# Page gathers of the sample cache spread over seven heads, and the first gate activation moved ahead in the weight loop

## What is computed

```
h = rms_norm(x, norm_pre);  z = h @ w_in      # c_q, c_kv, k_r, u_pool, u_conv, gate
o_lat = attend(q_abs, q_rope, c_kv, k_r)      # 8 heads; for the samples also over
                                              #   cache_ckv[page_table], cache_krope[page_table]
mixed = concat([o_att, y_pool, y_conv]) * silu(gate)
out   = x + rms_norm(mixed @ w_out, norm_post)
```

## Time and profile before

| | |
|---|---|
| median of 3 runs | 1404.8 us (1403.98 to 1406.93) |
| the profiled execution | 1409.98 us, of which 1408.2 us are the span |
| busy over the span | PE 91%, PE weight loads 75%, DVE 59%, ACT 44%, POOL 34% |
| stage 2 | about 455 to 944 us |
| stage 3 | 944 to 1010 us |
| stage 4 | 1010 us to the end |

### The profile page before, as it was taken

How to read it: one execution, slowest core, us unless ns; L and a number is a source line. 1 busy time by engine, 2 the same in 40 slices (tenths; PEclk the granted TensorE clock), 3 DMA queues, 4 the chain that set the end, 5 groups by cost and what they waited for, 6 DMA issues and landing times. The chain is left out here.

```text
span 1408.2 us, 21384 instructions
## 1 busy us (share of the span) xinstructions
PE 1285.1 (91%) x7456; PEld 1058.7 (75%) x7456; DVE 836.8 (59%) x1799; ACT 625.4 (44%) x1271; POOL 483.9 (34%) x420
## 2 busy tenths in 40 slices
PE   4889979989865899999999999959889999999998
PEld 3767758677534788888888888856568888888885
DVE  3468676686663888888888888834334232333312
ACT  5423142341421777777777777724242222221211
POOL 5236146352362235234152350008603232222312
PEclk9999999999975899999999999979999999999999
DMA  7534161241516032231231321637263131313221
GB/s 244 150 101 152 40 213 64 91 166 50 198 32 117 10 102 67 74 92 36 81 95 40 91 56 30 190 90 208 94 213 119 62 120 61 120 60 120 75 64 38
DMA packets 141696, 141.71 MB, mean 101 GB/s; under 512 B 55637, under 2 KB 110902, under 8 KB 140118
## 3 DMA queue, kind: packets, MB, share of 16 engines
q1 hardware_dynamic: 133350, 112.19, 27.2%
q0 software_dynamic: 5360, 17.68, 4.3%
q10 hardware_dynamic: 2880, 10.49, 2.3%
HBM read 104.08 MB, written 46.71 MB: 107 GB/s over the span
## 5 line engine op out<-in xcount | busy, mean ns | idle before, releaser
L1291 ACT ACTIVATE pT<-tp 128x512 fp32r<-128x512 f32 (+2 forms) x320 | 168.4, 531 | 116.9 <-PE tp L1230 107.9
L1348 DVE TENSOR_SCALAR_CACHE_REDUCE prob<-sc 128x512 f32<-128x512 f32 (+2 forms) x320 | 192.9, 603 | 31.6 <-PE sc L1222 17.7
L1357 DVE TENSOR_TENSOR big<-tp,pT 128x512 fp32r<-128x512 f32 (+2 forms) x320 | 193.9, 607 | 28.2 <-ACT pT L1291 27.8
L2006 PE MATMUL m<-w_gate,q2a 128*128 128x512 f32 x768 | 181.8, 396 | 3.5 <-POOLq L1984 3.5
L1230 PE MATMUL tp<-ident,prob 128*128 128x128 f32 x1088 | 171.9, 273 | 1.1 <-DVE big L1357 1.1
L1281 ACT ACTIVATE prob<-prob,nm 128x1024 f32<-128x1024 f32 (+2 forms) x192 | 171.7, 894 | 1.2 <-DVE nm L1351 0.7
L2006 PEld LDWEIGHTS m<-w_gate,q2a 128*128 128x128 f32 x768 | 145.5, 191 | 33.6 <-POOLq L1984 3.6
L701 DVE SCALAR_TENSOR_TENSOR acc<-aT,cols,acc 128x512 f32<-128x512 f32 x232 | 163.1, 751 | 10.2 <-DVE qst L777 0.9
L2168 DVE SCALAR_TENSOR_TENSOR shared<-m,rq,g_post 128x512 f32<-128x512 f32 x32 | 22.6, 747 | 232.0 <-POOL rq L1978 232.0
L1230 PEld LDWEIGHTS tp<-ident,prob 128*128 128x128 f32 x1088 | 128.8, 141 | 25.1 <-issue 1.7
L894 PE MATMUL mm<-big,w_in 128*128 128x512 f32 x576 | 141.8, 404 | 5.1 <-ACTq L585 5.1
(11 more groups left out here) (291 smaller groups left out, 2303.6 us busy)
## 6 DMA issues: line engine op xcount, KB each, us to landing
xtok<-in_x ACTq DMA_DIRECT2D x20, 512.0 KB, 4.5
xraw<-in_xT SPq DMA_DIRECT2D x17, 512.0 KB, 4.4
QT<-qst SPq DMA_DIRECT2D x32, 256.0 KB, 3.4
LAT<-in_cache_ckv SPq DMA_DIRECT2D x128, 64.0 KB, 2.1
k2a<-Y SPq DMA_DIRECT2D x16, 512.0 KB, 5.5
shared<-in_x SPq DMA_DIRECT2D x16, 512.0 KB, 4.4
out_y<-shared SPq DMA_DIRECT2D x16, 512.0 KB, 2.9
raw<-QT SPq DMA_DIRECT2D x7, 1024.0 KB, 5.1
```

The source lines that it names most:

```text
L1291: act.activation(pT[0][:, 4 * c:4 * c + w // P, (t % 4) * P:(t % 4 + 1) * P], tp[n % NTP][:, 0:w].rearrange("p (k q) -> p k q", q=P), ACT. ...
L1348: dve.tensor_scalar(prob[:, slot[m % J], 0:w], sc[b][:, 0:w], -1.0, None, ALU.mult, ALU.min, accum_out=top).then_inc(sc_free[b], 1)
L1357: dve.tensor_tensor(cut(1), tp[n % NTP][:, 0:w].rearrange("p (k q) -> p k q", q=P), f32(cut(0)), ALU.subtract)\
L2006: last = pe.matmul(out, w(pw_, k), x(px, k), start=(k == 0 and q == 0), stop=(k == n - 1 and q == 2))
```

## The change

The 128 pages are numbered through, over all samples, and dealt over 28 slots, the four groups of heads 0 to 6. A slot has 4 or 5 pages, head 7 none. The wait ahead of `load_first_pages` is now for all pages. In stage 4, `silu(0, 0)` and `divide(0)` stand ahead of chunk 2 instead of chunk 4.

```diff
-                def gather(b, pages):
-
-                    for pg in pages:
+                def gather(pages):
+
+                    for b, pg in (divmod(n, N_PAGES) for n in pages):
...
-                        parts = 4 if h < HEADS - 1 else 2
-                        if g < parts:
-                            gather(h, range(g * N_PAGES // parts, (g + 1) * N_PAGES // parts))
+                        at, slots = h * 4 + g, 4 * (HEADS - 1)
+                        if at < slots:
+                            gather(range(at * DEC_BATCH * N_PAGES // slots, (at + 1) * DEC_BATCH * N_PAGES // slots))
...
-                            sp.wait_ge(s["gather"], 32 * (DEC_BATCH - 1) * N_PAGES)
+                            sp.wait_ge(s["gather"], 32 * DEC_BATCH * N_PAGES)
...
                 for k in range(MC):
-                    if k == MC // 2:
+                    if k == MC // 4:
                         silu(0, 0)
...
                 for k in range(MC):
-                    if k == MC // 2:
+                    if k == MC // 4:
                         divide(0)
```

## The result

The changed kernel takes 1397.5 us (median of 4 runs, 1396.1 to 1398.4), against 1405.9 us for the kernel before. The ratio is 0.9943, with a 95% interval of 0.993 to 0.9956: 8.0 us faster, between 6.2 and 9.8. The forecast was 7.9 us.

A forecast was written before the change was run, and what follows sets the result against it. It took TensorE's nearly unbroken stage 4 stream to set the end, with holes in head 7 and at stage 4's start. -9.92 - 1.1 + 0 + 0.9 + 2.2 = -7.9 us, from 1404.8 to 1396.9 us; range 1392.0 to 1401.5.

The forecast's parts named there:

- Gathers out of head 7: Stage 2, head 7: without 8 pages ahead of group 0's store, VectorE's wait goes whole, -9.92 us, plus -1.1 us.
- the second term: Head 7: TensorE's lower clock behind the idle time goes too, -1.1 us, taken from between 0 and 2.
- The store isn't too late behind the loads: Head 7: group 0's store lands by 908.4 us, needed at 913.53; rival of a late store, 1401.9 us, chance 0.10.
- Heads 0 to 6 cost nothing: Stage 2: 16 more pages in heads 0 to 6 are covered, cost 0; without cover 32 us.
- V's gap on SP: Head 2: SP has 4.47 us between group 0's store and issuing V, covering a slot's growth of 2.03 us.
- the slower rival: Heads 0 to 6: longer slots delay V and TensorE waits, 1429 us, from 4.47 us of growth; chance 0.04.
- The silus: Start of stage 4: silus end 4.6 us earlier, but the output projection of tile 0 starts later and slower, +3.1 us.
- The slow stretch: Stage 4: after some 8 us idle, TensorE starts tile 0's output projection at half clock, +2.2 us.
- a gain of 7.4 us: Stage 4 rival: Y's load lands early enough that the gates' end decides, up to -7.4 us, 1386.4 us; chance 0.05.
- The offset: Whole kernel: the profiled execution lies 5.2 us above the median of the runs, taken as constant.
- the last two rivals: Longer slots delay V, 1429 us, chance 0.04; head 7's wait has another cause than SP's order, 1408 us, 0.02.
- the slower side: Whole kernel: chance that the change measures slower, given as 0.05.

The follow-up runs named there:

- silus_only: Kernel before with both silus moved ahead of chunk 2, nothing else: 1410.5 us, ratio 1.0025.
- hole_filled: Changed kernel with 30 unneeded matmuls added on TensorE between the gates of tile 1 and the first output projection: 1395.5 us, ratio 0.9921.
- four buffers: Changed kernel with silus back ahead of chunk 4 and the chunks of w_out loaded through four buffers instead of two: 1390.2 us, ratio 0.9881.
- four_buffers_early: Changed kernel, silus ahead of chunk 2, with four buffers for the chunks of w_out instead of two: 1395.7 us, ratio 0.9912.
- gathers_only: Changed kernel with both silus back ahead of chunk 4, so only the gathers are moved: 1397.2 us, ratio 0.9935 to the kernel before.
- slots_four_heads: Changed kernel with silus back ahead of chunk 4 and gathers dealt over four heads, 16 slots of 8 pages: 1446.95 us (one run).
- stores_before_gathers: Kernel before with each group's store in head 7 issued ahead of that group's page gathers: 1405.0 us, ratio 0.9991.
- slots_five_heads: Changed kernel with silus back ahead of chunk 4 and gathers dealt over five heads, 20 slots of 6 or 7 pages: 1396.1 us (one run).

## Why the prediction was right, and where it wasn't

**Gathers out of head 7: right.** Forecast -9.92 - 1.1 us, measured 10.9 to 11.0 us less of head 7 in each kernel that leaves no page there. That the second term came out is luck: I took 1.1 us from between 0 and 2, and no row fixed it. Two kernels tell the cause from its rivals: the wait goes when the store is put first, and comes back with 2.0 us when 4 pages are put ahead of it.

**The store isn't too late behind the loads: right, with less to spare than I had worked out.** SP gets to it at 899.80 us, 9.2 us ahead of the `ost` of group 2. I took 4.0 us for its landing, from the first gather, and it took 5.7 behind the 5 MB of loads. The reserve was 3.5 us instead of 5.1. The wait went whole all the same, so the sum wasn't hurt.

**Heads 0 to 6 cost nothing: right in the sum, wrong in its reason.** They take 425.6 to 427.9 us with the 28 slots and 427.1 to 427.4 without. The limit wasn't V's gap on SP: 7 pages passed it, for one wait of 1.2 us in the whole stage. What decides, as far as two kernels can tell, is whether SP's whole load fits into a head of 57.5 us: with 52 us of gathers it does, with 65 it takes 69 and doesn't, and the stores feel it first. My point of decision for the slower rival, 4.47 us of growth, was wrong.

**The silus: right.** They ended earlier, the hole moved behind the gates (8 us forecast, 7.85 measured), and the part costs. Forecast +0.9 and +2.2 us; measured +0.7 and +1.9 between the two kernels, and 2.3 us between the means over all. silus_only gives it by the time alone, 3.5 us (2.0 to 5.1). The slow stretch is shown by hole_filled. The later start of 0.7 us isn't, since it varies by 1.6 us between kernels with the same order, and its working was off: counted from the first gate matmul, SP issues the load of `Y` 1.6 us later (24.6 and 23.0 us), not 0.9, and it then lands 0.8 us sooner behind its issue. I named the load of `Y` as the thing that the projection waits for. It is the last to end, but taking it away gains nothing, since the chunks' chain ends only 0.9 us ahead of it. Of the rivals, a gain of 7.4 us was excluded because that chain had no slack, and with four buffers, where it has, the gain is there.

**The offset: wrong.** I took the 5.2 us between the profiled execution and the median as constant. It was mostly variation in stage 1: the changed kernel's profiled execution lay 0.6 us above its median, at 1398.1 us instead of the forecast 1402.1. The sum was made of differences within a stage, so it wasn't hurt. The cuts of the two traces give -11.0 + 2.6 = -8.4 us and the runs 8.0, between 6.2 and 9.8, so the forecast's 7.9 can't be told from either. A slip on the way: the last two rivals have 0.04 and 0.02, and I gave the slower side 0.05.

## What to carry to other kernels

An issuing engine that works in program order is a resource: count its time per step, and look for small urgent stores queued behind many transfers that have no hurry; then spread these over all steps that have room, since merely reordering them leaves their sum. Moving a wait up in an engine's order helps only if the work put behind it isn't what the next consumer waits for; before it is moved, ask which chain ends second, and by how little. And TensorE's idle time can cost twice: here 3.7 to 8.4 us of it at the start of stage 4 brought 1.6 to 2.7 us more at the lower clock, while up to 2.0 us brought nothing.

## What the runs showed of the hardware

- Behind 7.85 us of idle the granted clock stayed at 0.50 for about 4 us (changed kernel). A shorter hole wasn't cheaper: in four_buffers_early, with 3.69 us, the clock fell at 1027 us, about 1 us ahead of the projection, and stayed at 0.50 until 1033.8, 5.6 us behind the projection's start, and cost 2.6 us where the longer one cost 1.9. Across 0.75, 1.5 and 2.0 us of idle (gathers_only, hole_filled, slots_four_heads) it stayed at 1.00. Thirty matmuls of no use, 6.96 us long, won 1.9 us.
- Identical code in stage 1 ended anywhere between 447.5 and 455.7 us over twelve profiled executions, while the last 352.5 to 352.6 us of TensorE's stream repeated to 0.1 us. For a change of 2 us, a stage cut out of the trace was the sharper instrument than the median of the whole.
- A page costs SP about 2 us for its two transfers, of which the two issues are 0.49 us each: 1.93 us from page to page in the rows of stores_before_gathers, and the 2.03 of my sum has in it the longer first issue. This is the issuing engine's own time: with the DMA share at 0.20 from 918 to 933 us, 16 pages held up the end of the stage by 9.5 us.
- A store of 128 KB that took 2.4 us to land (median of the stage) took 5.7 to 6.3 us when it was issued right behind the 5 MB of loads (changed kernel, gathers_only, slots_five_heads, stores_before_gathers).
